# Half-split inverse, a bias table stored in parts, and a rewritten key-selecting attention in a two-block decoder kernel

## The reference, cut to what matters

```python
# first_block: h = concat(meta, x); layer 0 even_mixer, layer 1 swa_mixer,
#              each followed by h += conv_ffn(rms_norm(h))
def gated_delta_rule(q, k, v, beta, g):       # 4 heads of 128, chunks of the tokens
    a_strict = where(strict, beta * (k @ k.T) * dmask, 0)
    sol = triangular_solve(a_strict + eye(c), rhs)          # unit lower triangle
    ...
# second_block: layer 0 moba_attention, layer 1 dsa_attention, each then
#               x += square(relu(norm(x) @ w_up)) @ w_down
def dsa_attention(h, w_in, g_q, g_kv, w_uq, w_qi, w_uk, w_uv, w_o, bias_table):
    c_q, c_kv, k_idx, w_idx = split(h @ w_in, [256, 512, 576])
    c_q, c_kv = rms_norm_2(c_q, g_q), rms_norm_2(c_kv, g_kv)
    q_nope = c_q @ w_uq                      # 16 heads of 64
    q_idx = c_q @ w_qi                       # 8 index heads of 64
    score = sum_h w_idx[h] * relu(q_idx[h] @ k_idx.T)       # causal
    idx = top_k(score, 64)                   # the keys that each query may see
    logits = q_nope @ (w_uk c_kv[idx]) * 64 ** -0.5 + bias_table[rel_bucket(t - idx)]
    return (softmax(logits) @ (c_kv[idx] @ w_uv)) @ w_o
```

## Time and profile before

| | |
|---|---|
| median of 3 runs | 1341.94 us (1339.29 to 1344.5) |
| the profiled execution | 1342.86 us |
| its span | 1341.1 us, mean TensorE clock 0.974 |
| TensorE, VectorE, ScalarE, GpSimd busy | 95%, 68%, 49%, 15% |
| DMA | 206.31 MB, mean 154 GB/s |
| mix_in to the store's end | 0 to 162 us |
| dsa_in to dsa_out's first products | 1031 to 1125 us |

### The profile page before, as it was taken

One profiled execution on the slowest core, in us unless ns is written; L12 is line 12 of the kernel. 1 busy time (PEld: TensorE's weight loads), 2 busy tenths in 40 slices (PEclk: granted clock), 3 DMA queues, 4 the chain that ended last, 5 costly groups with the idle time before them and its releaser, 6 DMA issues.

```text
span 1341.1 us, 27354 instructions
## 1 busy us (share of the span) xinstructions
PE 1274.6 (95%) x10217; PEld 1227.4 (92%) x10217; DVE 905.8 (68%) x1684; ACT 662.6 (49%) x1163; POOL 197.9 (15%) x225
## 2 busy tenths in 40 slices
PE   7988889999999998999999999999999779999996
PEld 7868888999999887999999999999999757999996
DVE  7856327877754686888854776866556697876453
ACT  6543214555543465655544555655444376655331
POOL 0112204100011333200011002200012034200011
PEclk9978879999999998999999999999999899999998
DMA  7523713555554421665655544655557321665551
GB/s 257 158 75 69 121 33 109 180 175 175 189 190 149 132 86 54 198 186 180 215 196 169 168 142 138 207 183 181 187 188 235 110 64 52 200 184 182 184 188 63
DMA packets 60498, 206.31 MB, mean 154 GB/s; under 512 B 6016, under 2 KB 14464, under 8 KB 60288
## 3 DMA queue, kind: packets, MB, share of 16 engines
q1 hardware_dynamic: 56144, 200.81, 48.7%
q10 hardware_dynamic: 4272, 4.35, 1.0%
HBM read 200.95 MB, written 4.19 MB: 153 GB/s over the span
## 4 chain that ended last, share of the span: by engine, by line
PE 87%; DVE 8%; issue 2%; ACT 2%; DMA 0%; DVEq 0%; POOL 0%; POOLq 0%; ACTq 0%
PE bank L304 26%; PE bank L306 25%; PE bank L305 25%; DVE cb L646 1%; PE bank L1089 1%; DVE w_lo L265 1%; PE bank L1459 1%; PE bank L1105 1%; PE bank L1043 1%; PE bank L1481 1%; PE bank L1471 1%; PE bank L1103 1%; DVE sm_d L1336 1%; ACT w_hi L256 1%; DVE sm_d L1354 1%
## 5 line engine op out<-in xcount | busy, mean ns | idle before, releaser
L265 DVE TENSOR_TENSOR w_lo<-raw,w_hi 128x1024 fp32r<-128x1024 f32 (+1 forms) x358 | 458.0, 1280 | 209.9 <-ACT w_hi L256 208.9
L256 ACT ACTIVATE w_hi<-raw 128x1024 fp32r<-128x1024 f32 (+1 forms) x358 | 387.6, 1085 | 306.7 <-PE bank L306 287.3
L304 PE MATMUL bank<-x_hi,w_hi 128*128 128x256 f32 (+2 forms) x1784 | 515.7, 289 | 12.6 <-DVE x_lo L385 7.9
L306 PE MATMUL bank<-x_hi,w_lo 128*128 128x256 f32 (+2 forms) x1784 | 509.8, 286 | 0.0
L305 PE MATMUL bank<-x_lo,w_hi 128*128 128x256 f32 (+2 forms) x1784 | 509.6, 286 | 0.0
L304 PEld LDWEIGHTS bank<-x_hi,w_hi 128*128 128x128 f32 x1784 | 340.0, 191 | 17.4 <-DVE w_lo L265 10.4
L305 PEld LDWEIGHTS bank<-x_lo,w_hi 128*128 128x128 f32 x1784 | 339.1, 190 | 1.7 <-issue 1.4
L306 PEld LDWEIGHTS bank<-x_hi,w_lo 128*128 128x128 f32 x1784 | 339.8, 190 | 0.0
L304 PE MATMUL bank<-m_hi,w_hi 128*128 128x256 f32 x512 | 143.4, 280 | 0.0
L305 PE MATMUL bank<-m_lo,w_hi 128*128 128x256 f32 x512 | 142.8, 279 | 0.0
L306 PE MATMUL bank<-m_hi,w_lo 128*128 128x256 f32 x512 | 142.8, 279 | 0.0
(11 more groups left out here) (302 smaller groups left out, 1730.4 us busy)
## 6 DMA issues: line engine op xcount, KB each, us to landing
raw<-w_up SPq DMA_DIRECT2D x88, 512.0 KB, 3.5
raw<-w_mlp_up SPq DMA_DIRECT2D x64, 512.0 KB, 3.6
raw<-w_mlp_down SPq DMA_DIRECT2D x64, 512.0 KB, 3.9
raw<-w_down SPq DMA_DIRECT2D x32, 704.0 KB, 4.1
raw<-w_mix_in SPq DMA_DIRECT2D x29, 512.0 KB, 3.6
raw<-w_moba_in SPq DMA_DIRECT2D x24, 512.0 KB, 4.1
raw<-w_swa_in SPq DMA_DIRECT2D x12, 512.0 KB, 3.5
raw<-w_mix_out SPq DMA_DIRECT2D x8, 512.0 KB, 3.6
```

The costliest lines, as they stand in the source:

```text
L256: nc.scalar.activation(w_hi[:, slot, 0:WIDTHS[g]], raw[:, slot, 0:WIDTHS[g]], ACT.Copy).then_inc(hi_ready, 1)
L265: nc.vector.tensor_tensor(w_lo[:, slot, 0:WIDTHS[g]], raw[:, slot, 0:WIDTHS[g]], w_hi[:, slot, 0:WIDTHS[g]].bitcast(F32), ALU.subtract).th ...
L304: nc.tensor.matmul(out, whi, xh, start=(chunk == 0), stop=False)
L306: mm = nc.tensor.matmul(out, wlo, xh, start=False, stop=end)
```

## The change

**Mixer.** `ba` and `l2r` get 128 rows, cleared by GpSimd, and the broadcasts contract over all 128. From level 2 on only the even half of P's columns is computed and copied (`half(..., level, 0)`); GpSimd writes zeros into the odd halves that the level before filled (`odd_of`), and TensorE waits for them from level 3 on.

**Bias.** SP stores `rel_scratch` in eight parts of 16 rows of repeats, one after every four weight loads of up0. `bias_m` is loaded by ScalarE in the last pass of swa's pairs; `bias_d` in four parts during dsa_in.

**dsa.** The norms are taken in two groups with tokens on partitions, between dsa_in's tiles. The index tiles come first in dsa_q, and each tile can be evacuated by itself (`part_done`). Index scores lie between the query tiles. dsa_k keeps 8 key tiles; dsa_v makes the values token-major at once, 24 products of 512 columns into four banks. The attention runs as `Pairs`. The normalisation and the transposes are gone: VectorE multiplies the identity by the reciprocals (`diag`), and TensorE's product of the exponentials with that diagonal turns and scales in one (`turn`). GpSimd adds bias and mask for two heads at once. The first three tiles of dsa_out take their first five chunks (DSA_EARLY) in passes 8, 9 and behind them. A pass of the attention is, for VectorE, `pair_reduce(p)`, `diagonals(p - 1)`, `pair_low(p - 2)`.

```diff
@@ linears @@
-    ("dsa_in", 6, KD, 1, 1), ("dsa_q", 12, 2, 1, 4), ("dsa_kv", 16, 2, 1, 4),
+    ("dsa_in", 6, KD, 1, 1), ("dsa_q", 12, 2, 1, 4), ("dsa_k", 8, 2, 1, 4), ("dsa_v", 2, KD, 1, 1),
@@ act_mix, pool_mix @@
+                    act.wait_ge(S("cleared"), 4)
+                    nc.scalar.activation(half(p_of(n)[0:c, 0:w], level, 0), half(INV_BANKS[n][0][0:c, 0:w], level, 0),
+                                         ACT.Copy).then_inc(p_ready[n], 1)
...
+                if level >= 3 and n == (0 if level <= LEVELS[0] else 2):
+                    for m in (1, 2, 0):
+                        if level <= LEVELS[m]:
+                            pool.wait_ge(y_done[m], level - 2)
+                            nc.gpsimd.memset(odd_of(m, level - 1), 0.0).then_inc(S("odd_zero"), 1)
@@ pe_mix @@
-                rows = 36 if b < 8 else 8
-                nc.tensor.matmul(BC[b % 4][:, 0:T], ident[0:rows, col:col + 1].to_broadcast([rows, P]),
-                                 (ba if b < 8 else l2r)[0:rows, :], start=True,
+                nc.tensor.matmul(BC[b % 4][:, 0:T], ident[:, col:col + 1].to_broadcast([P, P]),
+                                 (ba if b < 8 else l2r)[:], start=True,
...
-                            mm = nc.tensor.matmul(pbank[0:c, hs], bt[0:c, n, hs], xm_of(n)[0:c, hs],
-                                                  start=True, stop=True)
+                            mm = nc.tensor.matmul(half(pbank[0:c, hs], level, 0), bt[0:c, n, hs],
+                                                  half(xm_of(n)[0:c, hs], level, 0), start=True, stop=True)
...
+                    if level >= 3:
+                        pe.wait_ge(S("odd_zero"), INVERSE.index((level, n)) - 5)
@@ act_swa @@
+                        act.wait_ge(S("rel_stored"), 16 * 8)
+                        load_bias(act, bias_m, 0, HEADS, S("bias_loaded"))
@@ dve_dsa @@
+            def diagonals(p):
+                for j in range(2):
+                    u = 2 * p + j
+                    dsa.wait(dve, "exp", 2 * u + 2)
+                    nc.vector.reciprocal(st_d[:, u, 6:8], st_d[:, u, 4:6]).then_inc(dsa.s["rec"], 1)
+                    dsa.wait(dve, "rec", u + 1)
+                    if p:
+                        dsa.wait(dve, "turned", 2 * p - 1 + j)
+                    nc.vector.tensor_tensor(
+                        diag[:, j, :, :], ident.unsqueeze(1).to_broadcast([P, 2, P]),
+                        st_d[:, u, 6:8].unsqueeze(2).to_broadcast([P, 2, P]),
+                        ALU.mult).then_inc(dsa.s["p"], 2)
+
+            for p in range(HEADS // 2 + 2):
+                if p < HEADS // 2:
+                    pair_reduce(dve, dsa, p, bias_ready)
+                if 1 <= p <= HEADS // 2:
+                    diagonals(p - 1)
+                if p > 1:
+                    pair_low(dve, dsa, p - 2)
@@ pool_dsa @@
-            for u in range(HEADS):
-                if u >= 2:
-                    dsa.wait(pool, "max", 2 * (u - 2) + 2)
+            for p in range(HEADS // 2):
+                u = 2 * p
+                pool.wait_ge(part_loaded[p // 2], 32)
+                if p >= 2:
+                    dsa.wait(pool, "max", 4 * (p - 1))
+                for c0, w, k0 in ((0, 2 * P, 0), (2 * P, P, P)):
+                    nc.gpsimd.tensor_tensor(
+                        b2[:, u % 4:u % 4 + 2, c0:c0 + w], bias_d[:, u:u + 2, k0:k0 + w],
+                        pick[:, c0:c0 + w].unsqueeze(1).to_broadcast([P, 2, w]),
+                        ALU.add).then_inc(S("b2_ready"), 1)
@@ pe_dsa @@
+            def turn(p):
+                for j in range(2):
+                    u = 2 * p + j
+                    dsa.wait(pe, "p", 2 * u + 2)
+                    if p:
+                        dsa.wait(pe, "pt", 2 * p - 1 + j)
+                    for dst, c, x in ((0, 2 * P, 1), (P, 0, 0), (2 * P, P, 0)):
+                        mm = nc.tensor.matmul(TURN_BANKS[j][:, dst:dst + P], dsa.slot(u)[:, c:c + P],
+                                              diag[:, j, x, :], start=True, stop=True)
+                    mm.then_inc(dsa.s["turned"], 1)
+
+            for p in range(HEADS // 2 + 2):
+                if p < HEADS // 2:
+                    pair_scores(pe, dsa, p)
+                if p == 0:
+                    pe.wait_ge(evac_done, v.tile0 + 2)
+                if p == HEADS // 2:
+                    pe_tile(pe, out, 0, ready=early, part=(0, DSA_EARLY))
+                if 1 <= p <= HEADS // 2:
+                    turn(p - 1)
+                if p > 1:
+                    if p == HEADS // 2 + 1:
+                        dsa.wait(pe, "max", 2 * HEADS)
+                        pe_tile(pe, out, 1, part=(0, DSA_EARLY))
+                    pair_values(pe, dsa, p - 2)
+            pe_tile(pe, out, 2, part=(0, DSA_EARLY))
@@ sp @@
-                if name == "mix_out":
-                    sp.wait_ge(S("rel_ready"), 1)
-                    sp.dma_start(rel_scratch, relv[:].unsqueeze(1).to_broadcast([HEADS, P, VLEN])
-                                 ).then_inc(S("rel_stored"), 16)
+                if name == "up0":
+                    sp.wait_ge(S("rel_ready"), 1)
+                    for part in range(8):
+                        for k in range(RING):
+                            load(lin, g + k)
+                        g += RING
+                        sp.dma_start(rel_scratch[:, HEADS * part:HEADS * (part + 1), :],
+                                     relv[:].unsqueeze(1).to_broadcast([HEADS, HEADS, VLEN])
+                                     ).then_inc(S("rel_stored"), 16)
```

More of the change, by code:

```diff
@@ L1154, in pe_mix @@
             for hd in range(4):
-                nc.tensor.matmul(bank[4 + hd][:, 0:T], ident[0:4, hd:hd + 1].to_broadcast([4, P]),
-                                 l2r[0:4, :], start=True, stop=True).then_inc(S("on_bc"), 1)
-        def store_rounds(eng, lin, slot):
-            for t in range(4):
-                slot(t, 0)
-            rounds = lin.tiles // 4 - 1
-            if rounds > 0:
-                with eng.Fori(0, rounds) as i:
-                    for t in range(4, 8):
-                        slot(t, i)
-            for t in range(4 * (rounds + 1), lin.tiles):
-                slot(t, 0)
@@ new lines, in reciprocals, with normed @@
+            def reciprocals(g):
+                dve.wait_ge(S("c_std_ready"), g + 1)
+                nc.vector.reciprocal(c_rec[:, 2 * g:2 * g + 2],
+                                     c_std[:, 2 * g:2 * g + 2]).then_inc(S("c_rec_ready"), 1)
+            def normed(g):
+                dve.wait_ge(S("c_spread"), g + 1)
+                for f in (2 * g, 2 * g + 1):
+                    nc.vector.scalar_tensor_tensor(
+                        out=ds_[:, f, :], in0=ds_[:, f, :], scalar=prm_col("g_kv" if g else "g_q", f % 2),
+                        in1=bank[5][:, SEQ * g:SEQ * (g + 1)], op0=ALU.mult,
+                        op1=ALU.mult).then_inc(S("c_ready"), 1)
+                for f in (2 * g, 2 * g + 1):
+                    dve.wait_ge(y_hi_ready, Y0["dsa_q"] + f + 1)
+                    nc.vector.tensor_tensor(y_lo[:, f, META:T], ds_[:, f, :],
+                                            y_hi[:, f, META:T].bitcast(F32),
+                                            ALU.subtract).then_inc(y_lo_ready, 1)
@@ new lines, in dve_dsa @@
+            for t in range(6):
+                dve_rest(dve, lin.piece0 + t + AHEAD)
+                if t == 0:
+                    dve_rstd(dve, name)
+                wait_tile(dve, lin, t)
+                nc.vector.tensor_tensor(ds_[:, t, :], tile_bank(lin, t)[:, 0:SEQ], rstd[:, 0:SEQ],
+                                        ALU.mult).then_inc(evac_done, 1)
+                if t == 3:
+                    reciprocals(0)
+                if t == 4:
+                    dve.wait_ge(evac_done, lin.tile0 + 2)
+                    normed(0)
@@ L2100, in dve_dsa @@
                     nc.vector.scalar_tensor_tensor(
[L2101 removed]
+                        out=score[:, c0:c0 + w], in0=rl[:, hd % 4, c0:c0 + w],
                         scalar=head_w[:, w0 + hd:w0 + hd + 1], in1=prev, op0=ALU.mult,
                         op1=ALU.add).then_inc(S("score_done"), 1)
[L2105 to L2106 removed]
+            dve_rest(dve, v.piece0)
             for r in range(TOPK // 8):
                 if r % 2 == 0:
[L2109 removed]
+                    dve_rest(dve, v.piece0 + 1 + r // 2)
                 for x, (c0, w, _) in enumerate(groups):
@@ new lines, in pe_dsa @@
+            pe.wait_ge(S("relu_done"), 8)
+            for c in range(2):
+                g = v.piece0 + c
+                slot = g % RING
+                pe.wait_ge(lo_ready, g + 1)
+                for b in range(4):
+                    tok, cs = META + P * (b // 2), slice(512 * (b % 2), 512 * (b % 2 + 1))
+                    xh, xl = y_hi[:, 2 + c, tok:tok + P], y_lo[:, 2 + c, tok:tok + P]
+                    nc.tensor.matmul(bank[4 + b][:], xh, w_hi[:, slot, cs], start=(c == 0), stop=False)
```

(10 more changed lines are left out.)

547 lines of the change are left out of this document (195 added, 352 removed).

## The result

The changed kernel takes 1354.4 us (median of 4 runs, 1353.56 to 1355.11) against 1340.93 for the kernel before on the same chip: ratio 1.0102, interval 1.0081 to 1.0122. It is 13.5 us slower, 1.0%, and each of its executions is longer than each of the kernel before; the forecast was 1340.0, its range ended at 1352. Of the experiments' executions one, the second of run 1, was slow (2075.71 us at a mean clock of 0.559) and is left out.

A forecast was written before the change was run, and what follows sets the result against it. TensorE, busy 95% of the span, was taken as the bound, so edits pay where it waits or runs at its lower clock. Terms -4.6, -8.8, -1.5, -10.0, +23 gave -1.9: 1341.0, less 0.9 for the median, 1340.0 us; range 1326 to 1352.

The forecast's parts named there:

- Part 1, broadcasts: Mixer: broadcasts over 128 rows raise TensorE's clock; -4.6 us in the sum, 0 if rows have no part.
- Part 2, store: Bias store in eight parts: removes two TensorE idles and the half clock behind them; -8.8 us.
- the slack of the ring: up0's weight loads: ring of four and early rounding give a tile or two of slack, so store parts cost 0.
- the load of bias_m: End of swa's pairs: the moved load costs 0, at most +3 us if swa_out's weights queue behind it.
- Part 3, halves: Mixer's inverse: half of P's columns saves 0.25 us on each of six levels; -1.5 us.
- Part 4, front of dsa: dsa_in to the mask: index part first brings the mask earlier; -10.0 us.
- Part 5, attention: dsa, mask to dsa_out: 59 us against 36.0, +23; +12 at full clock, +35 at half.
- The circle: dsa attention: engines wait for each other in a closed loop; a pass 5.5 us at full clock, 6.4 beside GpSimd.
- I take half of the passes at either: dsa attention: half the passes at full clock, half at the low one, giving 59 us, +23.
- my signs of being wrong: dsa attention: a pass under 5 us, or mask to dsa_out under 45 or over 72 us.
- Rival C: dsa attention never leaves the low clock, the state feeding itself; mean grant about 0.6, +35, 1352 us; chance 0.15.

The follow-up runs named there:

- run 1: The changed kernel with one more wait, so GpSimd's bias and mask sums start behind VectorE's diagonals from pass 3 on; 1342.31 us (one execution).
- run 7: The changed kernel with the mixer's broadcasts over 36, 8 and 4 rows again; 1352.97 us.
- run 8: The changed kernel with the bias stored in one DMA ahead of mix_out's weights again; two executions, 1352.77 and 1358.83 us.
- run 2: The changed kernel with six unused products on TensorE ahead of each turn in the attention; 1340.92 us.
- run 9: The changed kernel with eighteen unused products between the attention's first scores and first turn, as a warm start only; 1347.89 us.
- run 3: The changed kernel with values and next scores ahead of the turn on TensorE, and y_hi ahead of the copies on ScalarE; 1331.78 us.
- run 5: The changed kernel with values and next scores ahead of the turn, and GpSimd's sums behind the diagonals; 1327.23 us, ratio 0.9896 to the kernel before.
- run 4: The changed kernel with the attention of the kernel before, one head a step with normalisation and transposes; 1326.38 us, ratio 0.989 to the kernel before.

## Why the prediction was wrong

**What bounds the kernel.** Right: the time moved where TensorE waited or ran at its lower clock, and the other engines moved it only through such waits.

**Part 1, broadcasts.** Mechanism right (run 7). The first step of the sum came out well: the gram products come 5.7 us earlier behind mix_in's std, forecast 4.6. The 4.5 us that I gave the clock to come back stood on no row; in ten traces with full rows it came back 4.7 to 6.4 us behind the first of these products, in two it was not lost. The step that failed is that this is the end's gain. I never asked what is late next: VectorE's chain of gates comes only 2.8 us earlier, and TensorE waits 5.9 for `kd` where it waited 3.0. At the inverse's start 2.7 us were left of 5.7. Of the 3.4 us that the mixer's stage is off, this part makes 1.9 and part 3 makes 1.2.

**Part 2, store.** Right in mechanism. From the level 2 products to the inverse's end it was 54.95 us and is 45.89; less the 0.3 of the halves that is -8.8, the number forecast. That it fits so closely is partly luck: put back in run 8, the store cost 6.9 us there, since the idles and the half clock behind them differ from trace to trace. Up0 took the parts at nothing, as the slack of the ring said. swa_in to down1 is 1.75 us longer, where the load of bias_m had a price of 0 to 3. It is not the load: run 7 has the same load and 292.72 us for this stage, before it was 292.77. In the change 1.5 us are lost before the load is issued at 501 us, in a stretch at half clock (the first line), where before the same place of the stage had the full clock (the second):

```profile
449.60:452.80 3.20, 3.20 (x16) 3.20 (x15) 1.23 (x1) 1.16 (x2) 0.00 (x0) 0.50 0.00 0
```

```profile
460.20:463.40 3.20, 3.20 (x27) 2.98 (x28) 1.74 (x3) 1.70 (x3) 0.00 (x0) 1.00 0.00 0
```

Both come 2.6 us behind the same wait of 1.05 us. Why it took the clock in one and not in the other is open; in the other runs the stage takes 293.5 to 294.6.

**Part 3, halves.** Wrong by 1.2 us. The price came from rows of another product of 64 columns, 1.79 against 2.06. That difference is not one of columns: in both rows most records start 0.112 us apart, which sixteen times is 1.79, and 0.15 of the 0.27 us is a break between two groups of eight in the row of 2.06.

**Part 4, front of dsa.** -9.96 for -10.0. The terms: scores from 1048.5, that is 26.2 after the std where I had 26.3, the value tiles hidden as said, and TensorE idle ahead of the mask as said.

**Part 5, attention.** The circle, its members and VectorE's wait were right, and so were the lengths at either clock: 6.4 and 5.5 at full (6.80 and 5.78 in run 2), 8.7 and 7.8 at half (8.76 and 7.68 to 7.53). The step that failed is "I take half of the passes at either". The five passes ahead of the tail were all of the low length (8.76, 8.93, 8.60, 7.68, 7.53), and the stretch took +29.9 for +23. My reading of the mean grant was at fault as well: I let 0.6 decide, but with a mean of 0.67 most turns and values still ran at half clock (2.93 and 1.55 us; the shortest turn of the five passes took 2.26); the full clock was granted where TensorE waited and in some of the scores. In a circle only the grant in its own members counts. None of my signs of being wrong came up, since they bounded the circle and not the clock. Rival C had the length of the passes and most of the price, but not that the state feeds itself: run 9 left it with the gaps still there. Its +35 would have been 5 us too long, and what put the time past 1352 were terms that C did not have: the mixer's 3.4 us, 1.75 and 0.86, and that the median lies 0.8 above the profiled execution where I took 0.9 off. So C's 1352 lies near the result partly because errors cancel.

Ladder of the attention, by runs 2, 3, 5 and 4: 92.15, full clock 79.13 (-13.0), order 70.67 (-8.5), GpSimd out of the way 66.59 (-4.1), one head a step 63.49 (-3.1). What each is worth depends on the others: GpSimd's part was 4.1 at full clock and 9.9 in the change itself (one execution).

The Trainium skill's rule on the shared port pair ("SBUF — State Buffer", Who interferes with whom) held: the diagonal takes 1.33 us beside the addition, 0.42 without.

## What to carry to other kernels

When an attention is rewritten so that each engine's order has the next step behind a wait for another engine, write down the circle that closes and price it before counting saved instructions; then put the work that nobody waits for (values, next scores) ahead of the work that waits. Where a loop leaves TensorE a gap like the 3.3 us here in each pass, price it at the lower clock too; what is saved on another engine may then count more than once, and the time varies from execution to execution. A gain early in a chain ends at the next engine that is already late: look for the wait that grows.

## What the runs showed that was not expected

- TensorE's clock went by the rows of the products and not by its busy time alone: with 36 and 8 rows it was at 0.50 for 17.1 us of a stretch without idle time, with 128 rows for 6.8 us at most.
- The same wait takes the clock in one execution and leaves it in another: of fourteen traces, all with 3.2 us of idle TensorE ahead of the broadcasts, twelve lost the clock there and two (runs 3 and 5) kept it.
- Useless work made the kernel 13.5 us faster (run 2): a pass with 2.86 us of added products takes 6.80 us, without them 8.76.
- A product of 64 columns with its own weight load costs the same as one of 128: both start every 0.112 us.
- One wait more on GpSimd gained 9.9 us in the attention in the one execution there is, and 4.1 where the clock is full.
- The change's other parts with the attention of before, or with the new one reordered, are 1.1% faster than the kernel before: 1326.38 and 1325.84 us.
